# FFN 2's last projection as seven block products in three sweeps, with the residual put into the banks as sums of its corners

## What is computed

```python
def conv_ffn_2(xn, w_up, conv_w, conv_b, w_down):
    h = xn @ w_up                                  # 512 x 1024 @ 1024 x 5632
    ...                                            # causal convolution of width 3 over the tokens, + conv_b
    a, b = jnp.split(h, 2, axis=-1)
    return (jax.nn.silu(a) * b) @ w_down           # 512 x 2816 @ 2816 x 1024
...
h = h + conv_ffn_2(rmsnorm(h, norm_ffn_g[l]), w_up[l], conv_w[l], conv_b[l], w_down[l])
return rmsnorm(h, norm_final_g)
```

## Time and profile before

| | us |
|---|---|
| median of 3 runs (1619.11, 1620.76, 4057.6) | 1620.76 |
| profiled execution | 1619.13 |
| its span | 1617.3 |
| PE busy in the span | 1586.1 |
| DVE busy | 1020.2 |
| ACT busy | 651.9 |
| POOL busy | 198.0 |

### The profile page before, as it was taken

How to read it: one execution, slowest core, us unless ns; L and a number is a source line. 1 busy time by engine, 2 the same in 40 slices (tenths; PEclk the granted TensorE clock), 3 DMA queues, 4 the chain that set the end, 5 groups by cost and what they waited for, 6 DMA issues and landing times.

```text
span 1617.3 us, 20534 instructions
## 1 busy us (share of the span) xinstructions
PE 1586.1 (98%) x7826; PEld 1303.1 (81%) x7826; DVE 1020.2 (63%) x1416; ACT 651.9 (40%) x859; POOL 198.0 (12%) x132
## 2 busy tenths in 40 slices
PE   6999999999999999999999999999999999999998
PEld 5888788788887888888877877777888888888887
DVE  5569563458797677755886767777355555556233
ACT  5333453242234533333565522444544333334223
POOL 1110033110002011111100001430123011011000
PEclk9999999999999999999999999999999999999999
DMA  9332223118653288734544343212123333332221
GB/s 331 94 122 87 67 65 105 53 53 285 203 189 99 84 285 290 258 101 130 184 168 134 95 126 99 79 60 77 53 78 117 99 84 104 104 87 95 104 104 52
DMA packets 198554, 202.23 MB, mean 125 GB/s; under 512 B 10359, under 2 KB 177620, under 8 KB 197076
## 3 DMA queue, kind: packets, MB, share of 16 engines
q1 hardware_dynamic: 180560, 181.88, 35.8%
q10 hardware_dynamic: 16948, 16.89, 3.3%
q0 software_dynamic: 976, 2.51, 0.4%
HBM read 185.73 MB, written 13.63 MB: 123 GB/s over the span
## 4 chain that ended last, share of the span: by engine, by line
PE 90%; DVE 5%; ACT 2%; DMA 2%; issue 1%; SPq 0%; ACTq 0%; DVEq 0%
PE bank L1578 21%; PE bank L1580 20%; PE bank L1579 20%; PE bank L1593 4%; PE bank L1595 4%; PE bank L1594 4%; PE bank L2094 2%; PE bank L2096 2%; PE bank L2095 2%; PE bank L1680 1%; PE bank L2270 1%; DVE w_lo L2327 1%; PE bank L1923 1%; DMA w_raw<-in_w_in 1%; PE bank L1586 1%; DVE w_lo L2898 1%
## 5 line engine op out<-in xcount | busy, mean ns | idle before, releaser
L1578 PE MATMUL bank<-h_hi,w_hi 128*128 128x512 f32 (+1 forms) x1424 | 556.5, 391 | 4.2 <-DVE w_lo L2327 1.9
L1580 PE MATMUL bank<-h_hi,w_lo 128*128 128x512 f32 (+1 forms) x1424 | 548.2, 385 | 0.0
L1579 PE MATMUL bank<-h_lo,w_hi 128*128 128x512 f32 (+1 forms) x1424 | 547.8, 385 | 0.0
L2327 DVE TENSOR_TENSOR w_lo<-w_raw,w_hi 128x2048 fp32r<-128x2048 f32 x101 | 236.6, 2343 | 189.5 <-ACT w_hi L900 188.8
L1578 PEld LDWEIGHTS bank<-h_hi,w_hi 128*128 128x128 f32 x1424 | 267.6, 188 | 73.2 <-issue 15.7
L1580 PEld LDWEIGHTS bank<-h_hi,w_lo 128*128 128x128 f32 x1424 | 267.7, 188 | 53.9
L1579 PEld LDWEIGHTS bank<-h_lo,w_hi 128*128 128x128 f32 x1424 | 267.8, 188 | 52.5 <-issue 1.0
L900 ACT ACTIVATE w_hi<-w_raw 128x2048 fp32r<-128x2048 f32 x118 | 225.2, 1908 | 184.2 <-PE bank L1595 101.8
L792 POOL TENSOR_TENSOR w_lo<-w_raw,w_hi 128x2048 fp32r<-128x2048 f32 x17 | 79.3, 4664 | 487.7 <-ACT w_hi L900 487.7
L829 POOL TENSOR_TENSOR work<-work 128x512 f32 x44 | 58.8, 1335 | 438.1 <-ACT work L1334 438.1
L1326 ACT ACTIVATE work<-work,par 128x512 f32<-128x512 f32 x44 | 35.8, 815 | 106.8 <-DVE work L2954 106.8
(11 more groups left out here) (352 smaller groups left out, 2243.5 us busy)
## 6 DMA issues: line engine op xcount, KB each, us to landing
w_raw<-in_w_in SPq DMA_DIRECT2D x94, 512.0 KB, 4.7
w_raw<-in_ffn_w_up SPq DMA_DIRECT2D x44, 512.0 KB, 5.0
w_raw<-in_w_up SPq DMA_DIRECT2D x44, 512.0 KB, 4.9
work<-in_ada_w ACTq DMA_DIRECT2D x16, 1024.0 KB, 7.7
work<-in_ffn_w_down SPq DMA_DIRECT2D x28, 512.0 KB, 5.8
down_sums<-work SPq DMA_DIRECT2D x11, 1024.0 KB, 4.9
w_raw<-in_w_down SPq DMA_DIRECT2D x22, 512.0 KB, 3.7
work<-in_ada_w SPq DMA_DIRECT2D x8, 1024.0 KB, 12.6
```

Of the source, the lines that this page charges most:

```text
L1578: pe.matmul(dst, w_hi[s][:, at:at + n], hi, start=first, stop=False, skip_group_check=onto)
L1579: pe.matmul(dst, w_hi[s][:, at:at + n], lo, start=False, stop=False, skip_group_check=onto)
L1580: return pe.matmul(dst, w_lo[s][:, at:at + n], hi, start=False, stop=last, skip_group_check=onto)
L2327: dve.tensor_tensor(w_lo[u % 2][:, :], raw[u % 2][:, :], w_hi[u % 2][:, :].bitcast(FP32), ALU.subtract)\
```

## The change

FFN 2 takes FFN 1's scheme. The functions of the seven products get the FFN's name as an argument, and their semaphore counts an offset.

- PE: `down_unit` goes, and FFN 2 runs the three sweeps: 264 + 132 + 66 = 462 matmuls in the place of 528. The 32 transposing matmuls stay and put corners of `x` into the banks.
- DVE: four new operations (`x_corners`, each on 128 x 1024) turn the four corners of `x` (two halves of the channels by two halves of the tokens) in place into the sums that the banks need; they stand between the first and the second step of the up projection. `down_sums` (three operations) stands in units 2 to 12 of FFN 2's up projection, between the next unit's low part and the scaling. `inner_sums`, `inner_lo` and the low parts of the 20 units follow as in FFN 1. In FFN 2 the second unit's low part stands ahead of the last taps.
- POOL: the difference in each pair (L842) in FFN 2 too.
- ACT: the high parts of hidden blocks and of 20 units, four copies out of the banks (`aside`). `down_hi(1)` stands ahead of the last unit's centre taps.
- SP: the loads and stores of the weight sums in FFN 2's up projection, and the 20 units' loads.
- Both FFNs: the four places of raw weights are taken in another order. Units 0 and 1 use `w_raw`, units 2 and 3 use it again, and units 4 and 5 the areas of `work`. So unit 2's load waits for unit 0's low part, also in FFN 1.
- The end: the first two row groups are finished beside sweep 3. In the last sweep banks 4 and then 6 get the last products; banks 5 and 7 are ready before.

The diff, cut to its core:

```diff
-                        ("ga", 4), ("ya", 2), ("wo2", 4), ("up2", FT), ("down2", FT // 2)]:
+                        ("ga", 4), ("ya", 2), ("wo2", 4), ("up2", FT), ("down2", DOWN_UNITS)]:
...
+        DOWN = {n: U["down" + n] for n in BEFORE}
+        SLOT = {n: [(g if g < 2 else (g - 2) % 4) ^ first % 2 for g in range(DOWN_UNITS)] for n, first in DOWN.items()}
 
         def place(u):
 
-            g = u - DOWN
-            return g % 4 if 0 <= g < DOWN_UNITS else u % 2
+            for n, first in DOWN.items():
+                if first <= u < first + DOWN_UNITS:
+                    return SLOT[n][u - first]
+            return u % 2
...
+                    sp.wait_ge(sem("sums_made"), 3 * (BEFORE[n] * PAIR + p + 1))
+                    sp.dma_start(kept[n][p], sum_slot(p)).then_inc(sem(f"sums_kept{p % 2}"), 16)
+
+                for i in range(PAIR):
                     for k in range(2):
                         up_unit(i, k)
-                row_unit(U["down" + n], w_down, 0)
-                with sp.Fori(0, FT // 4) as i:
-                    for k in (1, 2):
-                        row_unit(U["down" + n] + k, w_down, i * (4 * P) + k * 2 * P, i)
+                        p = 2 * i + k - 4
+                        if 1 <= p <= PAIR:
+                            sums_store(p - 1)
+                        if 0 <= p < PAIR:
+                            sums_load(p)
+                down_rows(n, w_down)
...
+            def down_rows(n, w_down):
+
+                for g in range(DOWN_UNITS):
+                    u, dst, pairs = DOWN[n] + g, raw_at[SLOT[n][g]], PAIRS_OF[g]
+                    if g == 0:
+                        for k in range(2):
+                            sp.wait_ge(sem(f"sums_kept{k}"), 16 * (kept_by(n, k) + (PAIR + 1 - k) // 2))
+                    if g < 2:
+                        before(u)
+                    elif g in (4, 5):
+                        sp.wait_ge(sem("hid"), (BEFORE[n] + 1) * (FT + 1))
+                    else:
+                        v = u - 2 if g < 4 else u - 4
+                        sp.wait_ge(parted[v % 2], v // 2 + 1)
+                    if g < PAIR:
+                        r = g * 2 * P
+                        put(u, dst[:, 0:S], w_down[r:r + P, 0:S])
+                        put(u, dst[:, S:4 * S], kept[n][g][:, S:4 * S])
+                    elif g < THIRD:
+                        for q in range(2):
+                            m = len(pairs) * S
+                            p, c = divmod(q * m, D)
+                            r = (2 * (pairs[0] + p) + 1) * P
+                            put(u, dst[:, q * m:(q + 1) * m], w_down[r:r + P, c:c + m])
+                    else:
+                        for a, b in ((0, 2), (2, len(pairs))):
+                            put(u, dst[:, a * S:b * S].rearrange("p (a n) -> p a n", a=b - a),
+                                kept[n][pairs[0] + a:pairs[0] + b].rearrange("a p n -> p a n")[:, :, 0:S])
 
             w, w2 = A["w_in"][0], A["w_in_2"][0]
 
...
                 pool.nop().then_inc(sem("hid"), 1)
-                if n == "2":
-                    with pool.Fori(0, PAIR) as i:
-                        for k in range(2):
-                            tile(i, k)
...
                         elif not begun:
                             split(up + k + 1, i * 2, 2)
                         if last:
-                            (inner_hi if n == "1" else part_hi)(k)
+                            inner_hi(n, k)
+                        if last and k and deferred:
+                            down_hi(n, 1)
...
                                            scale=par[:, bass.ds(i * 2 + at, 1)], **kw).then_inc(sem("center"), 1)
-                        if last and k and n == "1":
-                            down_hi(1)
+                        if last and k and not deferred:
+                            down_hi(n, 1)
...
-                    return
-                split(down + 1)
-
-                split(down + 2)
-                part_hi(2)
-                with act.Fori(0, 4) as i:
-                    for d in (2, 3):
-                        split(down + d + 1, i * 2, 2)
-                        part_hi(d + 1, i * 2)
-                if down + FT // 2 < N_UNITS:
-                    split(down + FT // 2)
+                inner_hi(n, 2)
+                for g in range(1, THIRD):
+                    down_hi(n, g + 1)
+                    if g + 2 < DOWN_UNITS - 1:
+                        inner_hi(n, g + 2)
+                    if g == PAIR - 1:
+                        aside(0, 0)
+                        aside(0, 1)
+                    if g == PAIR:
+                        aside(4, 0)
+                        aside(4, 1)
+                        log_and_exp()
 
             ffn("1", ("ffn_dw_w/0", "ffn_dw_w/1", "ffn_dw_w/2"), None)
...
+            final_squares(0)
+            down_hi("2", THIRD + 1)
+            final_factor(0)
+            final_squares(1)
+            final_factor(1)
+            inner_hi("2", THIRD + 2)
+            down_hi("2", THIRD + 2)
+            for tt in (2, 3):
+                final_squares(tt)
+                final_factor(tt)
             act.wait_ge(sem("fin_rstd"), TT)
...
                             if g == 0:
-                                wait_free(pe, T["down1"][c + 2 * m])
+                                t = T["down" + n][c + 2 * m]
+                                wait_free(pe, t)
+                                if deferred:
+                                    for k in range(4):
+                                        pe.matmul(bank[t.bank][:, k * P:(k + 1) * P], x_corner(c, k, m), ident, start=k == 0, stop=False,
+                                                  is_transpose=True, skip_group_check=True)
                             mm = product(g, m, part, weight, c)
                         if g == PAIR - 1 and m == 0:
                             mm.then_inc(sem("first_done"), 1)
@@ -2115,9 +2085,9 @@
...
+                def x_corner(c, k, m):
+
+                    tile = k + (4 if c in (1, 4) else 0)
+                    at = m * P + (HALF if c in (1, 5) else 0)
+                    return x[:, tile, at:at + P]
+
+                for g in range(PAIR):
+                    down_ready(g)
+                    if g == 0 and deferred:
+                        pe.wait_ge(sem("x_ready"), 6 * KT + 4)
+                    first_products(g)
+                for g in range(PAIR, THIRD):
+                    down_ready(g)
+                    second_products(g, ((0, 0), (0, 1), (1, 0), (1, 1)) if g < THIRD - 1 else ((0, 0), (1, 0), (0, 1), (1, 1)))
+                for g in range(THIRD, DOWN_UNITS):
+                    down_ready(g)
+                    third_products(g, 0)
+                    if g == DOWN_UNITS - 2 and not deferred:
+                        rows_turned("down1", "res", 0)
+                    third_products(g, 1)
...
+            def x_corners():
+
+                r11, r12 = (x[:, 0:4, half_of(b)] for b in range(2))
+                r21, r22 = (x[:, 4:8, half_of(b)] for b in range(2))
+                for k, (out, a, b, op) in enumerate(((r21, r21, r22, ALU.subtract), (r22, r22, r12, ALU.add),
+                                                     (r12, r11, r12, ALU.subtract), (r12, r12, r21, ALU.add))):
+                    if k:
+                        dve.wait_ge(sem("x_ready"), 6 * KT + k)
+                    dve.tensor_tensor(out, a, b, op).then_inc(sem("x_ready"), 1)
 
...
-                        if last and k and n == "1":
-                            inner_lo(1)
-                            down_low(0)
+                        if last and k:
+                            inner_lo(n, 1)
+                            down_low(n, 0)
                             inner_sums(2)
                         elif not begun:
                             lo(up + k + 1, i * 2)
-                            if last and n == "1":
+                            if last:
                                 inner_sums(0)
                                 inner_sums(1)
-                                inner_lo(0)
+                                inner_lo(n, 0)
                         if sums and k < sums:
                             down_sums(i, k)
-                        if last and n == "2":
-                            part_lo(k)
                         if deferred:
                             for part in range(2):
                                 t = T["up2"][2 * k + part]
                                 wait_full(dve, t, i)
                                 release(dve.tensor_tensor(scaled[:, k, part, :], bank[t.bank][:, :], rstd[:, :], ALU.mult), t)
+                            if last and k:
+                                down_low(n, 1)
                         for tap in (1, 0):
...
-                    lo(down + FT // 2)
+                if n == "2":
+                    x_corners()
+                with dve.Fori(1, 6) as i:
```

(19 more changed lines are left out.)

324 lines of the change are left out of this document (97 added, 227 removed).

## The result

The changed kernel takes 1625.6 us (median of 6 runs, 1625.14 to 1631.67); the kernel before, on the same chip, 1621.62. The ratio is 1.0033 with an interval of 1.0017 to 1.0049: the same by 2%, and slower by about 4 us where the prediction had 0.4 us over the runs shown and 2.1 over the profiled execution. One of the six executions of before took 4057.6 us, far off all others; without it their median is 1620.76 and the change costs 4.8 us. The profiled execution of the changed kernel takes 1625.17, 6.0 us more than that of before.

What follows compares the result with a forecast made beforehand. PE was taken to bound the kernel, with DVE next: 1619.13 - 15.0 + 9.9 + 1.95 + 0.2 + 3.55 + 0.2 + 1.25 = 1621.2 us. Likeliest case (0.60) 1617 to 1626; 8 in 10 range 1611 to 1630.

Steps and rivals of the forecast that it cites:

- matmuls removed: PE in FFN 2's last projection: 66 fewer matmuls at 0.2267 us each, -15.0 us.
- up projection: FFN 2's up projection: weight sums make DVE's round 11.78 us against PE's 10.88, and corners delay its start; +9.9 us.
- hand-over: From FFN 2's up projection to the last projection: first weight unit's low part comes late, +1.95 us.
- unit 2: Last projection: unit 2's low part, queued behind taps and two `inner_lo`, is ready only just in time; +0.2 us.
- sweeps: Last projection's sweeps: stalls as in FFN 1, +3.55 us, and +0.2 for slow first matmuls after the stall.
- behind the last matmul: Kernel's end: last output starts 3.1 us after the last matmul, before 1.86; +1.25 us.
- ahead of FFN 2: FFN 1: unit 2's load now waits for a low part but still lands in time; 0, bounds -0.3 and +1.5.
- the rounds add up: FFN 2's up projection: ten DVE rounds with sums, each 0.90 us over PE's on average, show in full as PE gaps.
- (b): FFN 2's up projection: the sums' transfers end the round, DVE waiting for a DMA in each; 1630 us, chance 0.13.
- (a): FFN 2's up projection: the sums are hidden as in FFN 1, so the 9.9 goes; 1611.3 us, chance 0.18.
- (c): Whole gain: sums and boundaries hidden, only the end longer; some 1606 us, chance 0.05.
- (d): FFN 2's up projection: stalls in each round pull PE's clock down to 0.91, costing 11 us; 1632 us, chance 0.04.

Runs made afterwards that it cites:

- e4: Changed kernel with the counted loops of FFN 2's up projection written out on DVE and ACT, nothing else: 1623.55 us, 1.002 of before.
- e3: Changed kernel with POOL's difference of the hidden blocks in FFN 2 left out: 1622.12 us, 1.0004 of before.
- e2: Changed kernel with DVE's three operations of each FFN 2 weight sum left out, loads and stores kept: 1614.04 us, 0.9959 of before.
- e5: Changed kernel with two of three sum operations moved ahead of the low part, into DVE's wait for ACT, their load issued first: 1622.37 us.
- e8: e5 plus corners behind units 13 to 19, last projection's first block work two steps sooner, banks 5 and 7 squared first at the end: 1616.21 us.
- e9: e8 with SP's order in FFN 2's up projection changed to weights, load of sums, store of sums: 1635.63 us, 1.0099 of before.
- e10: e8 with SP's order as in the changed kernel, weights, store, load: 1651.66 us, 1.0186 of before.
- e12: e9 with the remaining counted loops of FFN 2's up projection written out on DVE and ACT: 1637.07 us, 1.0093 of before.
- e13: Changed kernel, sums' and SP's order kept, with loops written out, corners later, first block work earlier, end reordered: 1617.79 us, 0.9979 of before.

## Why the prediction was right, and where it was off

The forecast's mechanism and its range held: same by 2%, and 1625.6 in 1617 to 1626, though only 0.4 below its upper end, with the sum 4.4 us low. That the class would be "same" tests little, since the removed matmuls are worth 0.93% whatever eats them; the terms test more. On the profiled executions:

| term | predicted | measured |
|---|---|---|
| matmuls removed | -15.0 | -15.0 by count |
| up projection | +9.9 | 16.13 - 1.99 = +14.1 |
| hand-over | +1.95 | 2.22 - 0.23 = +1.99 |
| unit 2 | +0.2 | 0: no gap |
| sweeps | +3.75 | 111.67 - 123.20 + 14.96 = +3.4 |
| behind the last matmul | +1.25 | 7.2 - 5.9 = +1.3 |
| ahead of FFN 2 | 0 | +0.2 |
| sum | +2.1 | +6.0 |

**The up projection** is the mis-sized term, and in it two pieces of measured length that were taken from the wrong place. The first: "from the first scaling to the first tap 1.63". That row is of a step outside the counted loop; inside it ACT's tap comes 0.2 later, and e4 gives those 0.2 back. With it and 0.06 of rest the round is 12.04 instead of 11.78, 10 x 0.26 = 2.6 us. The second: the corners, "1.26 each, 5.0 in all". They took 6.39, because POOL's product and difference of the same step run at that time and both engines slow each other: 1.4 us. Of that, e3 shows 0.4 for the difference by leaving it out; that the other 1.0 is the product's is read from the times at which the two meet, and a corner that met nothing, the first or the last, took 1.22. 9.9 + 2.6 + 1.4 = 13.9 of 14.1, so the up projection ended at 1504.5 where 1500.2 was forecast. The signs of it were in the rows: the prediction charged POOL's difference to the low part (0.52, confirmed by e3) and didn't ask what else POOL would fall on.

**That the rounds add up** was right, and e2 shows it: without the operations 12.5 of the 16.1 go, with the transfers in place. The gaps came in turn (0.7 and 1.0 idle; 0.6 and 1.2 were predicted, and by the distance between starts, less the usual 0.23, 0.84 and 1.20 came), DVE's wait for PE went, and the DVE wait for data that rival (b) asks for did not appear.

**The boundaries** were right to a few tenths, since FFN 1 shows them: 1.67 idle ahead of unit 17, as in the earlier trace rows, 1.83 at the hand-over. The hand-over came as summed, 1.99 for 1.95. The distance from the last projection's first matmul to its last, 111.67 against the stated 112.5, and FFN 1's, within 0.03 of before, gave no sign of being wrong. The end was right: the last output starts 3.1 us behind the last matmul (1616.19 and 0.23 to 1619.54).

**The rivals.** (a) was wrong: the waits in DVE's round could not be filled by the order as it is; e5 shows that they can by another, at a price. (b) was wrong for this kernel: its loads land 7.7 us behind the sums before them, the wait would begin at 8.6. As a mechanism it came where DVE's own round was brought near 11 us: there DVE waits for loads up to 4.7 us. (c) needed what e2 leaves out. (d) fell for the changed kernel: the granted clock is 1.00 over twelve stalls of up to 1.4 us, and over the 1.83 and 1.67 us behind them. The Trainium skill's section on a second HAM failure mode (TensorE: Matmul & The Clock Gate) describes a clock that goes back and forth over short idle spells. The short waits here don't show it, longer ones do: the lower level came with waits of 2.2 to 4.6 us in e5, e8, e9, e10 and e12, not each time (e9 has four of 2.5 to 2.7 without it), and with none under 2.2 in FFN 2 of any run.

## What to carry to other kernels

When an engine's order is written by hand, compare its round with the bound engine's round, not its busy share: 12.04 against 10.88 was a loss on each of ten rounds, with DVE busy 80% of them. Take each piece of that round from a step of the same kind (inside the loop, with the same neighbours on the other engines), since 0.2 us is lost ten times over. Before moving work into a wait, follow what it reads back through the in-order queue that loads it, and look at the waits it makes on the way for a fall of the clock: here a saving of 1 us a round put a load into a loop of 12 to 15 us, and the plain edits of e13, which leave that queue alone, gave as much.
